# Sparse attention: key mask added on TensorE and row sums applied through diagonals; expert rows turned on VectorE

## What is computed

```python
idx_score = einsum(relu(q_idx . k_idx), w_idx)          # 16 index heads of 32
_, sel = top_k(where(causal, idx_score, -inf), 128)
logits = q . k[sel] * 64**-0.5 + rel_bias[bucket(q_pos - sel)]
p = softmax(where(sel <= q_pos, logits, -inf))          # 8 heads of 64
out = p @ v[sel]
```

```python
y[tok] += weight * ((silu(h[tok] @ gate[e]) * (h[tok] @ up[e])) @ down[e])
```

## Time and profile before

| what | value |
|---|---|
| median of three executions | 2505.81 us (2502.83 to 2510.84) |
| the profiled execution | 2498.72 us |
| its span in the profile | 2496.8 us, 25,488 instructions |
| mean granted clock of TensorE | 0.953 of full speed |
| moved by DMA | 446 MB, 179 GB/s over the span |

### The profile page before, as it was taken

One profiled execution on the slowest core, in us unless ns is written; L12 is line 12 of the kernel. 1 busy time (PEld: TensorE's weight loads), 2 busy tenths in 40 slices (PEclk: granted clock), 3 DMA queues, 4 the chain that ended last, 5 costly groups with the idle time before them and its releaser, 6 DMA issues. The chain is left out here.

```text
span 2496.8 us, 25488 instructions
## 1 busy us (share of the span) xinstructions
PE 2275.4 (91%) x9835; PEld 1130.6 (45%) x9835; DVE 862.4 (35%) x1468; ACT 485.3 (19%) x937; POOL 385.9 (15%) x755
## 2 busy tenths in 40 slices
PE   6998988999998998999967999888879999999985
PEld 3443654443443443444334488535434444444432
DVE  3456843222221130001888533423711111111116
ACT  2013552111110011001235422101011111111111
POOL 0004000400000000000000000000044444444424
PEclk9999999999999998998868999998989999999997
DMA  8502002455424113981202100302089999899867
GB/s 365 208 37 82 29 1 90 154 196 181 146 86 156 47 68 127 382 312 47 76 9 91 63 3 3 135 34 84 1 352 394 413 383 375 335 415 376 360 254 284
DMA packets 68553, 446.42 MB, mean 179 GB/s; under 512 B 12227, under 2 KB 12883, under 8 KB 43505
## 3 DMA queue, kind: packets, MB, share of 16 engines
q0 software_dynamic: 36176, 254.42, 25.8%
q1 hardware_dynamic: 32290, 190.78, 19.8%
HBM read 416.27 MB, written 73.45 MB: 196 GB/s over the span
## 5 line engine op out<-in xcount | busy, mean ns | idle before, releaser
L2533 PE MATMUL psum<-arena 128*64 128x512 f32 (+1 forms) x1088 | 360.6, 595 | 0.8 <-DMA arena<-in_exp_gu,arena 0.8
L938 PE MATMUL psum<-arena 128*128 128x512 f32 x704 | 307.2, 596 | 3.3 <-PEq L870 3.3
L2533 PEld LDWEIGHTS psum<-arena 128*64 128x64 f32 (+1 forms) x1088 | 138.8, 164 | 186.1 <-issue 185.1
L938 PEld LDWEIGHTS psum<-arena 128*128 128x128 f32 x704 | 133.3, 191 | 177.2 <-issue 177.2
L2524 PE MATMUL psum<-arena 128*64 128x512 f32 (+1 forms) x544 | 186.2, 598 | 1.2 <-ACT arena L2566 1.2
L1177 PE MATMUL psum<-arena 128*128 128x512 f32 x384 | 166.9, 597 | 3.6 <-ACTq L1228 3.6
L1068 PE MATMUL psum<-arena 128*128 128x512 f32 x352 | 153.5, 598 | 7.0 <-PEq L157 7.0
L997 DVE SCALAR_TENSOR_TENSOR arena<-psum,arena 128x511 f32<-128x511 f32 x88 | 66.0, 750 | 253.3 <-ACT arena L972 251.7
L2594 DVE TENSOR_TENSOR arena<-arena,psum 128x256 f32<-128x256 f32 x51 | 21.5, 421 | 342.0 <-ACT arena L2562 342.0
L833 PE MATMUL psum<-arena 128*128 128x512 f32 x256 | 113.0, 601 | 8.8 <-DMA arena<-in_w_out 8.1
L2524 PEld LDWEIGHTS psum<-arena 128*64 128x64 f32 (+1 forms) x544 | 68.5, 163 | 113.2 <-issue 111.8
(11 more groups left out here) (508 smaller groups left out, 2956.7 us busy)
## 6 DMA issues: line engine op xcount, KB each, us to landing
scratch_expert_out<-arena SPq DMA_DIRECT2D x18, 2048.0 KB, 18.6
scratch_expert_out<-arena SPq DMA_DIRECT2D x51, 512.0 KB, 9.3
arena<-in_w_ada SPq DMA_DIRECT2D x12, 2048.0 KB, 16.7
arena<-in_ada_w POOLq DMA_DIRECT2D x12, 2048.0 KB, 8.4
arena<-in_w_up SPq DMA_DIRECT2D x22, 1024.0 KB, 4.8
arena<-in_w_in SPq DMA_DIRECT2D x9, 2048.0 KB, 9.1
arena<-in_w_down SPq DMA_DIRECT2D x5, 2048.0 KB, 8.2
arena<-in_w_o SPq DMA_DIRECT2D x2, 2048.0 KB, 8.2
```

Source lines behind the costliest of these rows:

```text
L938: last = pe.matmul(K.bank[2 * (n % 3) + half], w[:, k, P * half:P * half + P], K.h[:, k, :], start=(k == 0), stop=(k == KD - 1))
L2533: last = pe.matmul(K.bank[2 + s][r, :], xt[:, s, P * k + r.start:P * k + r.stop], gu[:, lane, 2 * E_FF * k:2 * E_FF * (k + 1)], start=(k = ...
```

## The change

In sparse attention:
- The mask tile stays 1 or 0; its scaling by -1.0e30 goes. ScalarE makes a scaled identity `never` once. For tiles 1 to 3, `scores` accumulates a further product onto each head's bank, `never` times the mask tile, after waiting for the mask.
- The normalization of the probabilities goes. VectorE takes only the reciprocal; POOL multiplies the identity by it for both heads into `shares`, [128, 2, 128], double-buffered; `turn` becomes a plain product of the probability block with this diagonal, so that turning and normalizing are one.

In the expert phase:
- TensorE no longer turns gathered rows, and ScalarE no longer copies them. VectorE waits for the gathered rows and turns them straight into `xt` with 16 transpositions of 32-partition strips: each takes 8 blocks of 32 by 32. TensorE waits for that before its gate/up products. POOL's gather waits for the same signal.

```diff
+    shares, never = sb("shares2", [P, 2, 2, P]), sb("never2", [P, P])
+    inverted, never_out = sig("sums_inverted"), sig("never_ready")
...
-                                     K.z[a:a + 64, ZK + p, 0:keys(qt)], start=True, stop=True)
+                                     K.z[a:a + 64, ZK + p, 0:keys(qt)], start=True, stop=(qt == 0))
+                if qt:
+                    pe.wait_ge(never_out.sem, 1)
+                    pe.wait_ge(cut.sem, qt)
+                    for h in range(2):
+                        last = pe.matmul(K.bank[2 * (n % 2) + h][:, 0:keys(qt)], never[:, :], masked[qt - 1][:, :], start=False, stop=True)
                 s_mm.by(last)
...
+                pe.wait_ge(ex.sem, 2 * n + 2)
                 pe.wait_ge(pn.sem, n + 1)
...
-                        last = pe.transpose(K.bank[4 + h][:, P * k:P * k + P], prob[:, n % 2, h, P * k:P * k + P], K.ident[:, :])
+                        last = pe.matmul(K.bank[4 + h][:, P * k:P * k + P], prob[:, n % 2, h, P * k:P * k + P], shares[:, n % 2, h, :], start=True, stop=True)
...
+            never_out.by(act.activation(never[:, :], K.ident[:, :], ACT.Copy, scale=-1.0e30))
...
+            for n in range(UNITS):
+                pool.wait_ge(inverted.sem, n + 1)
+                if n >= 2:
+                    pool.wait_ge(t_pe.sem, n - 1)
+                pn.by(pool.tensor_tensor(shares[:, n % 2, :, :], K.ident[:, :].unsqueeze(1).to_broadcast([P, 2, P]),
+                                         rsum[:, 2 * n:2 * n + 2].unsqueeze(2).to_broadcast([P, 2, P]), ALU.mult))
...
-                link(dve, dve.tensor_tensor(m[:, :], left[:, 0:w], score[:, 0:w], ALU.is_equal), K.dve_step)
-                link(dve, dve.tensor_scalar(m[:, :], m[:, :], -1.0e30, None, ALU.mult), cut)
+                link(dve, dve.tensor_tensor(m[:, :], left[:, 0:w], score[:, 0:w], ALU.is_equal), cut)
...
-                if qt:
-                    link(dve, dve.tensor_tensor(x, x, masked[qt - 1][:, :].unsqueeze(1).to_broadcast([P, 2, w]), ALU.add), K.dve_step)
...
-                link(dve, dve.reciprocal(rsum[:, 2 * n:2 * n + 2], rsum[:, 2 * n:2 * n + 2]), K.dve_step)
-                x = prob[:, n % 2, :, 0:w]
-                pn.by(dve.tensor_tensor(x, x, rsum[:, 2 * n:2 * n + 2].unsqueeze(2).to_broadcast([P, 2, w]), ALU.mult))
+                inverted.by(dve.reciprocal(rsum[:, 2 * n:2 * n + 2], rsum[:, 2 * n:2 * n + 2]))
...
-                for k in range(KD):
-                    last = pe.transpose(K.psum[:, P * k:P * k + P], xg[:, b, P * k:P * k + P], K.ident[:, :])
-                last.then_inc(turned.sem, 1)
...
-                turn_x(i, s, 1)
+                blocks_done(pe, turned, i, s, 0)
...
-                act.activation(xt[:, (s + off) % U, 0:512], K.bank[0], ACT.Copy).then_inc(xt_act.sem, 1)
...
-                blocks_done(dve, turned, i, s, off)
+                b = (s + off) % U
+                landed(dve, x_in, i, s, off)
+                if isinstance(i, int) and i == 0 and s + off == 0:
+                    dve.wait_ge(cleared.sem, 1)
                 blocks_done(dve, gu_mm, i, s, off - U)
-                dve.tensor_copy(xt[:, (s + off) % U, 512:D], K.bank[1]).then_inc(xt_dve.sem, 1)
+                tokens, channels = xg[:, b, :].rearrange("p (k c) -> p k c", c=P), xt[:, b, :].rearrange("p (k t) -> p k t", t=P)
+                for a in range(0, P, 32):
+                    for c in range(0, P, 32):
+                        last = dve.transpose(channels[c:c + 32, :, a:a + 32], tokens[a:a + 32, :, c:c + 32])
+                last.then_inc(turned.sem, 1)
```

More of the change, by code:

```diff
@@ L1475, in logits @@
                                                    op0=ALU.mult, op1=ALU.add), lg)
-                if qt:
-                    link(dve, dve.tensor_tensor(x, x, masked[qt - 1][:, :].unsqueeze(1).to_broadcast([P, 2, w]), ALU.add), K.dve_step)
                 mx.by(dve.tensor_reduce(nmax[:, 2 * n:2 * n + 2], x, AX.X, ALU.max, negate=True))
             def norm(n):
-                w = keys(n // PAIRS)
                 dve.wait_ge(ex.sem, 2 * n + 2)
-                link(dve, dve.reciprocal(rsum[:, 2 * n:2 * n + 2], rsum[:, 2 * n:2 * n + 2]), K.dve_step)
-                x = prob[:, n % 2, :, 0:w]
-                pn.by(dve.tensor_tensor(x, x, rsum[:, 2 * n:2 * n + 2].unsqueeze(2).to_broadcast([P, 2, w]), ALU.mult))
+                inverted.by(dve.reciprocal(rsum[:, 2 * n:2 * n + 2], rsum[:, 2 * n:2 * n + 2]))
             for n in range(UNITS + 1):
@@ L1491, in _ @@
                     norm(n - 1)
-    K.memory.release("iw", "masked1", "masked2", "masked3", "top", "nmax2", "rsum2", "v2", "toe", "gate_w")
+    K.memory.release("iw", "masked1", "masked2", "masked3", "top", "nmax2", "rsum2", "shares2", "never2", "v2", "toe", "gate_w")
 C = P
@@ L2447, in phase_experts @@
     x_in = [K.dma_signal(f"e_x_landed{s}") for s in range(U)]
-    turned, xt_act, xt_dve = sig("e_x_turned"), sig("e_xt_by_act"), sig("e_xt_by_dve")
+    turned = sig("e_x_turned")
     gu_mm, silu, product = sig("e_gu_summed"), sig("e_silu"), sig("e_product")
@@ L2541, in step @@
                 last.then_inc(h_turned.sem, 1)
-            turn_x(0, 0, 0)
             steps(pe, step, lambda n: down_products(n, U))
@@ L2547, in _ @@
         def _(act):
-            def move_x(i, s, off):
-                blocks_done(act, turned, i, s, off)
-                blocks_done(act, gu_mm, i, s, off - U)
-                act.activation(xt[:, (s + off) % U, 0:512], K.bank[0], ACT.Copy).then_inc(xt_act.sem, 1)
             def move_out(i, s):
@@ L2558, in step @@
             def step(i, s):
-                move_x(i, s, 1)
                 blocks_done(act, gu_mm, i, s, 0)
@@ L2573, in rest @@
                     act.activation(g[:, 0, s:s + 1], K.rstd[:, 0:1], ACT.Copy)
-            move_x(0, 0, 0)
             steps(act, step, rest)
```

## The result

The changed kernel takes 2490.88 us (median of five, 2481.41 to 2493.82) against 2502.83 for the kernel before in the same session (five, 2497.92 to 2510.84). The ratio is 0.9948, 95% interval 0.993 to 0.9967: 12 us faster, clear of noise, and a third of the 39 us forecast. The profiled execution has a span of 2483.4 us, 13.4 less than before.

What follows compares the result with a forecast made beforehand. TensorE was taken to bound the expert stage and VectorE the sparse loop. Expert rows -44 + 12 - 4 = -36 us and sparse attention -3 gave -39: 2466.8 us from a median of 2505.81, range 2448 to 2494.

Steps and rivals of the forecast that it cites:

- 44 us removed from TensorE: Expert stage: 51 steps each lose 0.87 us of TensorE's row transpositions, all on the path.
- 16 transpositions in 5.6 us, hidden: Expert step: VectorE's new transpositions, 0.35 us apart, cost zero because up to some 9 us is hidden behind TensorE's products.
- I take 12: Expert stage: DMA becomes late next in full three-step stretches and takes back 12 us of the gain (bounds 4 and 30).
- Rival (a): DMA holds the whole expert stage, the landing margin failing in ordinary stretches too: total about -18 us, 2488; chance 0.14.
- Start of the stage, -4: Expert stage's first products wait for block 0 alone, its weights, landing about 1823, being the limit: gain 4 us (0 to 6).
- Sparse loop, -2 (3 - 1 - 4), with -1.1 for masks: Sparse attention: +3 us slow-clock units, -1 at the drain, -4 shorter waits; mask scaling removed before the loop saves 1.1.
- -4, a judgement: Sparse loop: some gaps are waits for TensorE at 1.2 GHz, which a steadier TensorE shortens by 4 us.
- Rule against row: Sparse loop's turning: by the skill's rule products cost 9 us more on TensorE; by profile rows only excess over VectorE's pace counts.
- part 2: The sparse-attention half of the change, forecast at -3 us in all, bounds -8 and +43.
- (b): Sparse loop turns TensorE-bound at 1.2 GHz for half its length: +15 us there, total about -22, 2484; chance 0.13.
- (c): VectorE's transpositions in the expert step are dearer, binding above 0.58 us each; at 0.69, 2541 us; chance 0.06.
- (d): VectorE's SBUF-to-SBUF transpositions hold up POOL's load issues, gate/up loads going out 5 us later: 2539 us; chance 0.07.

Runs made afterwards that it cites:

- Early loads: Changed kernel with POOL issuing each block's gate/up load ahead of the down load before it and the gather, same bytes: 2463.68 us, ratio 0.9841.
- the diagonals alone: Kernel before with only the normalization by diagonals from POOL, the mask staying on VectorE: 2505.80 us, sparse loop 71.6 us.
- the mask alone: Kernel before with only the mask added by TensorE, the normalization staying on VectorE: 2494.03 us, sparse loop 63.4 us.
- the copy first: Kernel before with both sparse edits, ScalarE's copy of turned probabilities queued ahead of exp: 2499.68 us, loop 66.8; with only the normalization by diagonals, 2491.43 us, loop 58.8.

## Why the prediction was wrong

The sign was right and the time lies within the range (2448 to 2494), but 12 us came where 39 were forecast. In the profiles the shortfall is 39 less 13.4, some 26 us: 18 in the DMA term and 8 in the sparse loop, the other terms and the stretches not touched cancel. By its steps:

- **44 us removed from TensorE.** Right. A step without waits is 10.8 us for 11.7, and without the down loads the stage loses 42.6 us.
- **16 transpositions in 5.6 us, hidden.** The size was off: 7.17 us, 0.448 apart and 0.436 each, with no overlap between independent ones, which the 96-element row had suggested. Hidden all the same, the cover of "some 9 us" held, but for one product that came 2.5 us late at the start, block 1's rows having landed only at 1831.8 (0.9 late before).
- **"I take 12" for DMA.** This is the step that failed. It measured 30, the upper bound: 22 of waits for weights, 3.4 of clock after two of them, the rest small. The pricing was by throughput: full triples at 425 GB/s lose 2.2 us each. The same paragraph had the right quantity, 15.7 us to land against a median of 12.5 and a maximum of 20.6, and drew from it only that prefetch could not smooth much. It was 14.6 us, since three sets of transpositions, 2.6 us, lie between what releases POOL (2103.80) and the need (2127.82), and the prediction took off two. Whenever a landing exceeded what a load had, the step paid the difference, in triples at a share of 1.00 as in some below it (0.88 at 2272 to 2306). The trace before held the answer: take each gate/up load's own landing there (for instance 17.0 us for the one issued at 2110.55, which had 17.3) and shorten its time to need by 2.6 us, and by this estimate 16 blocks miss by 21 us together, 13 of them blocks that did wait. Measured were 16 waits and 22 us. Early loads with equal bytes brought back 23 us. Rival (a) was this mechanism, and its 2488 the nearest price; it had 0.14, argued down by the mean rate of 371 GB/s. A mean rate says nothing about the load that is issued last and needed first.
- **Start of the stage, -4.** It was -5.3, near by luck: 1812.33 and a median landing of 12.5 make 1824.8, not the "about 1823" of the prediction, but that load lands after 8.8 us in the trace before (8.5 after). The limit was block 0's transpositions, begun at 1820.96 when its rows land, and not the weights.
- **Sparse loop, -2 (3 - 1 - 4), with -1.1 for masks.** This step failed too, by a smaller sum. The masks gave -1.3. The loop gave +5.8. Right: TensorE takes over at the same pace at full width (5.1 to 5.6 us, forecast 5.2), POOL's product at 0.61 us for 0.6, the clock at 0.97 or more from 1288 to 1334. Wrong: "-4, a judgement" for waits that a steadier TensorE would shorten (the twelve wide units gave -0.8, +0.9 and +0.4 by width, with the +3 for slow ones included), and "-1" at the drain (+2.0: turning twice as many passes at the lower level, behind the copy of the unit before). The first four units were not charged at all: +3.4, from twice the turning passes and the first masks at 1.2 GHz (the diagonals alone give +1.4 there, the mask alone +2.0). What I had not seen is ScalarE's order: it holds up the loop with the diagonals alone by 12.8 us. With both edits it costs 4.8, mostly at the drain, and with the copy first the loop still takes 66.8 us for 65.8 before.
- **Rule against row.** The Trainium skill, "Perfetto Trace Analysis", Transposes, says to use the transposition for a logical transposition; priced as in the prediction it made part 2 +6. The sparse part alone measured +2.8 us (0 to 5.5), with +5.8 in the loop. The rule was nearer than my sum. The fastest loop, 58.8 us, goes against it and still turns by real products; whether it would be faster yet with transpositions and the copy first, no run shows.
- **Rivals (b), (c) and (d).** Each is excluded by the trace. (b)'s 2484 lies near the result, but its mechanism did not come: the clock is 0.50 only in the first four units and low again only at the drain. The transpositions, 0.448 us apart, are below (c)'s 0.58. POOL's issues from the end of the down products to the last gate/up load take 6.75 us in the trace after (2070.05 to 2076.80), the same as before (2103.80 to 2110.55), beside 7.17 us of transpositions from SBUF to SBUF that begin at 2070.60.

## What to carry to other kernels

When a faster engine shortens a loop, don't price its transfers by rate alone: take for each load the time from issue to need, subtract the shortening, and compare it with that load's own landing in the trace, not with the median (here this gives 21 us of waits for 22 measured); then look whether the load could be issued as soon as its buffer is free. Moving work off the busiest engine may bring nothing, or a loss, where a ring through another engine's queue order is as long; write that ring out before choosing how much to move. Where two edits each shift load to the same engine, one of them may be worth more than both (the mask alone 63.4 us, both 71.6).

## What the runs showed of the hardware that was not expected

- Independent 32 x 256 transpositions on VectorE do not overlap: 0.436 us each, 0.448 apart, where eight independent 96-element operations of 0.32 us stand 0.25 apart. Each transposition writes another strip of 32 partitions than the one before; no run shows whether that or the operation itself is the reason.
- With early loads the DMA engines held 422 to 427 GB/s through four triples of 32.2 us in which TensorE never waited for weights (at 1964, 2097, 2194 and 2226); a share of 1.01 did not mean that anything was late.
- Two of the sixteen waits, of 2.06 and 2.95 us, cost a further 1.7 us each in the block behind them, TensorE being back at its 1.2 GHz level for part of it; behind the other fourteen, blocks kept their 7.1 us.
